# A fused two-block kernel on one core: value projection by channels with a turn behind it, one inverse application of 128 columns, an output turn in another bank, and a re-cut filling order

## Chip, cores, metric

One core of one Trainium2 chip. The metric is device time in microseconds (us) of one execution. Everything is float32.

## What is computed

The reference has a first block (an RWKV-7 layer, then a Hyena layer) and a second block (retention, differential attention and a gated MLP, two layers). The change touches the RWKV-7 layer alone. With 512 tokens (256 latent, 256 context) and 32 heads of 64 channels, cut to what matters here:

```python
proj = h @ w_in + (h_shift - h) @ (w_in * mu_cols)      # r, k, v, gate of 2048 channels each
kk = k * k_k; kk = kk / max(||kk||, 1e-12)              # per head of 64
# per head, in both directions z, one token after the other:
sa = s @ a_t                                            # a = -kk, b = kk * a
s  = s * w_t + sa b_t^T + v_t k_t^T
y  = s @ r_t
# both directions are added; then group norm per head, an affine, + bonus * v, * silu(gate)
```

The kernel evaluates the recurrence in chunks of 64 tokens. In a chunk, `sa` for all tokens is the solution of a triangular system whose 64x64 inverse is built by doubling.

## The kernel before

The layer runs as 16 rounds (`KE = 16`, called pairs here: one pair of heads, 128 channels, each). All engines' programs are written out by hand with semaphores; there is no planner. TensorE's program (`pairs_pe`) for pair `i` is a chain of small blocks in 64x64 tiles of the array, with full-array pieces for pair `i + 1` laid between them as fill:

- `first_blocks`, `low`, `full_blocks`: the chunk products; VectorE masks them (`start_inverse`, `mask_context`, `mask_tokens`).
- five levels of doubling: `below(l)` (64 matmul records in the trace), VectorE's `mask_level`, `grow(l)` (64 records), VectorE's `add_level`, then `turn_inverse` (DVE transposes) and ScalarE's `move_inverse`, and so to the next level. `seen_values` comes before the last `grow`.
- `solve`: the inverse times `W.AT` (the turned reads), then, in another group, times `W.X0` (the seen values): 32 matmuls of 64 columns each time. VectorE copies the first result (`weights`), ScalarE the second (`solved`).
- `transitions`, `own_states`, `own_reads`, then seven state steps `advance`/`read_states`, each round-tripping through VectorE and ScalarE (`state`).

The fill is the generator `between(i)`: it turns keys (`turn_keys`) and reads (`turn_reads`), projects the next pair's keys (8 matmuls of 512 columns), turns the previous pair's output (`turn_out`), and projects the next pair's values, reads and gates. `fill(part, columns)` takes pieces until their declared columns reach `columns`; the constants `FILL_*` say how much goes where. Each `pe.matmul` in float32 shows as two MATMUL records in the trace (8 key matmuls of 16 pairs: 256 records).

Values are projected with tokens as output rows: `mix_v` is the stationary operand and the weights are streamed, 32 matmuls of 128 columns (64 records) into bank 1. Bank 1 is also where `turn_out` puts the turned output of the pair before, which VectorE's `affine` reads; so `value_pieces` waits for `affine`. VectorE's `floor(m)` (the lower bound on the key norm, out of bank 0) stands behind the last `add_level`, and the first read piece waits for it because it writes bank 0.

DMA: each of the four weight slots (`w_k, w_v, w_r, w_g`, 512 KB) is refilled by the SP queue when its projection is done.

Of the kernel before, what the change touches and what calls it, by code (L numbers as in the profile page):

```python
# [14 lines left out]
P = 128  # L15
# [135 lines left out]
def rwkv_layer(nc, R, I, S):  # L151
# [19 lines left out]
    W.dif = hv[:, 6, :]  # L171
    W.late = [W.t1[0], W.dif]
    W.r, W.graw = hv[:, 7, 0:NX], hv[:, 7, NX:]
    W.t2 = [sv[:, 0, :], sv[:, 1, :]]
# [15 lines left out]
    W.Ax, W.Ac = sb("A_x", 2, 2, 4, P), sb("A_c", 2, 2, 4, HEAD)  # L190
    W.BK, W.AT, W.VZ = sb("BK", 2, NCH, P), sb("AT", 2, NCH, HEAD), sb("VZ", 2, NCH, P)
    W.T, W.U, W.Y, W.X0 = sb("T", 2, NCH, 64), sb("U", 2, NCH, 64), sb("Y", 2, NCH, 32), sb("X0", 2, NCH, 64)

# [193 lines left out]
def start_pool(pool, R, W, s):  # L387
# [32 lines left out]
LAST = 5  # L420
FILL_MASKS = 1000
FILL_BELOW = (0, 1000, 1000, 1000, 1100, 500)
FILL_GROWN = (0, 1200, 800, 800, 800, 800)
FILL_SEEN = 500
FILL_SOLVED = 500
FILL_MOVES = 500
# [98 lines left out]
def pairs_pe(pe, R, W, S, s, Z):  # L525
# [37 lines left out]
    def value_pieces(m):  # L563
        pe.wait_ge(s["w_v"], 16 * (m + 1))
        if m > 1:
            pe.wait_ge(s["affine"], 2 * (m - 1))
        if m == 0:
            pe.wait_ge(rate[1], 1)
            pe.wait_ge(s["mixed"], MIXED_V)
        for j in range(4):  # L570
            for k in range(KD):
                mm = pe.matmul(ps[:, 1, j * P:(j + 1) * P], W.mix_v[:, k, j * P:(j + 1) * P], W.wt[:, 1, k, :],  # L572
                               start=(k == 0), stop=(k == KD - 1))
                if k == KD - 1 and j == 3:
                    mm.then_inc(s["v_done"], 1)
                if k % 2:
                    yield

# [40 lines left out]

    def turn_out(i):  # L620
        pe.wait_ge(s["normed"], i + 1)
        pe.wait_ge(s["bonus_out"], i + 1)
        for j in range(2):
            pe.transpose(ps[:, 1, j * P:(j + 1) * P], W.ytok[:, j, :], R.eye[:, :])
        for j in range(2):
            mm = pe.transpose(ps[:, 1, NX + j * P:NX + (j + 1) * P], W.bonus[:, j, :], R.eye[:, :])
        mm.then_inc(s["turned"], 1)

    def bonus_weights(i):
# [4 lines left out]
        mm.then_inc(s["coef_done"], 1)  # L634

    def second_bank(i):
        if i + 1 < KE:
            pe.wait_ge(rate[1], i + 2)
        else:
            pe.wait_ge(s["g_out"], KE)  # L640

    def between(i):
        m = i + 1
        ahead = m < KE
        keys = key_pieces(m) if ahead else iter(())
        key = lambda: 512 if next(keys, None if not ahead else 1) is None else 0
        for z in range(2):
            for half in range(2):
                turn_keys(i, z, half)
                yield 290  # L650
            yield key()
        yield key()
        turn_reads(i)
        yield 640
        for _ in range(3):
            yield key()
        if i:
            second_bank(i)
            turn_out(i - 1)
# [7 lines left out]
        if not i:  # L667
            second_bank(i)
# [93 lines left out]
    def seen_values(i):  # L762
        for z in range(2):
            pe.wait_ge(v_in[z], i + 1)
            pe.wait_ge(at_out[z], i + 1)
        pe.wait_ge(s["coef_out"], i + 1)
        for j in range(4):
            for h in range(2):
                for p in range(2):
                    r, ch = nat(p), chunk_of(j, p)  # L770
                    for z in range(2):
                        g, n = solved_in(z, p), (4 * h + j) * 64
                        mm = pe.matmul(ps[g:g + 64, 6 + z, n:n + 64], strict(z, h, ch, r), W.VZ[r:r + 64, z, ch, rows(h)],
                                       start=True, stop=True)
                        if (j, h, p) == (3, 1, 1):
                            mm.then_inc(Z("x0_done")[z], 1)

    def solve(i, part):
        for z in range(2):
            pe.wait_ge(u_out[z], 6 * (i + 1))  # L780
        for n, right, done in ((0, W.AT, Z("wa_done")), (1, W.X0, Z("wu_done"))):
            if n:
                fill(part, FILL_SOLVED)
                for z in range(2):
                    pe.wait_ge(x0_out[z], i + 1)
            for j in range(4):
                for h in range(2):
                    for p in range(2):
                        a = oth(p)
                        for z in range(2):  # L790
                            g, q = solved_in(z, p), 4 * h + j
                            mm = pe.matmul(ps[a:a + 64, 2 + 2 * z + n, q * 64:q * 64 + 64], W.U[g:g + 64, z, q, :], right[g:g + 64, z, q, :],
                                           start=True, stop=True)
                            if (j, h, p) == (3, 1, 1):
                                mm.then_inc(done[z], 1)

# [67 lines left out]
    start_gate(pe, R, s, 2)  # L864
    start_gate(pe, R, s, 3)
    norm(0)
    for n, _ in enumerate(read_pieces(0)):
# [3 lines left out]
    for i in range(KE):  # L871
# [14 lines left out]
        for l in range(1, LAST + 1):  # L886
# [9 lines left out]
            fill(part, FILL_GROWN[l])  # L896
        solve(i, part)
        fill(part, FILL_SOLVED)
# [21 lines left out]
    pe.wait_ge(s["coef_out"], KE)  # L920
    turn_out(KE - 1)
    modulation_step(pe, R, S, 1, 1)


def pairs_act(act, R, W, s, Z):
# [45 lines left out]
    def root(m):  # L971
# [3 lines left out]
        act.activation(W.nrm, W.nrm, ACT.Exp, scale=-0.5).then_inc(s["root"], 1)  # L975

    def values(m):
        act.wait_ge(s["v_done"], m + 1)
# [23 lines left out]
    def reads_turned(i, z):  # L1002
        act.wait_ge(s["at_done1"], i + 1)
        act.activation(W.AT[:, z].rearrange("p (h j) n -> p h (j n)", h=2), ps[:, 6:8, z * NX:z * NX + NX], ACT.Copy).then_inc(Z("at_out")[z], 1)

# [7 lines left out]
    def seen(i, z):  # L1013
        act.wait_ge(Z("x0_done")[z], i + 1)
        if z:
            act.wait_ge(s["u_out1"], 6 * i + LAST)
        act.activation(W.X0[:, z].rearrange("p q n -> p (q n)"), ps[:, 6 + z, :], ACT.Copy).then_inc(Z("x0_out")[z], 1)

    def solved(i, z):
        act.wait_ge(Z("wu_done")[z], i + 1)  # L1020
        for p in range(2):
            g = slice(oth(p), oth(p) + 64)
            out = W.VZ[g, z].rearrange("p (j q) (h n) -> p h j q n", q=2, n=64)[:, :, :, p, :]
            src = ps[g, 3 + 2 * z, :].rearrange("p (h j n) -> p h j n", h=2, n=64)
            act.activation(out, src, ACT.Copy).then_inc(Z("u0_out")[z], 1)
# [25 lines left out]
    for z in range(2):  # L1051
        decays_early(0, z)
        decays_late(0, z)
    values(0)
    root(0)
    reads(0)
    gates(0)
    for i in range(KE):
# [32 lines left out]
        if ahead:  # L1091
            root(m)
        solved(i, 0)
        solved(i, 1)
# [12 lines left out]
def pairs_dve(dve, R, W, s, Z):  # L1107
# [100 lines left out]
    def weights(i, z):  # L1208
        dve.wait_ge(Z("wa_done")[z], i + 1)
        dve.tensor_copy(W.Wm[:, z].rearrange("p q n -> p (q n)"), ps[:, 2 + 2 * z, :]).then_inc(Z("w_out")[z], 1)  # L1210

# [39 lines left out]
    def affine(i):  # L1251
        vec = W.pv[:, i % 3, :]
        dve.wait_ge(s["turned"], i + 1)
        dve.tensor_scalar(W.yt, ps[:, 1, 0:NX], vec[:, V_LNW:V_LNW + 1], vec[:, V_LNB:V_LNB + 1], ALU.mult, ALU.add).then_inc(s["affine"], 1)
        dve.wait_ge(s["affine"], 2 * i + 1)
        dve.tensor_tensor(W.yt, W.yt, ps[:, 1, NX:], ALU.add).then_inc(s["affine"], 1)  # L1256

# [26 lines left out]
    for i in range(KE):  # L1284
# [9 lines left out]
        for l in range(1, LAST + 1):  # L1294
# [1848 lines left out]
```

## Time and profile before

| what | value |
|---|---|
| median of 3 runs | 2675.58 us (2672.11 to 2675.94) |
| profiled execution, its own time | 2679.32 us |
| its span, first to last instruction | 2677.5 us |
| mean granted TensorE clock | 0.988 of full speed |
| TensorE (PE) busy | 95% of the span |
| VectorE, ScalarE, GpSimd busy | 41%, 28%, 15% |
| the 16 pairs | from about 102 to 1076 us of the span |
| HBM read | 252.23 MB, 95 GB/s over the span |

Matmuls are pipelined and their ends are modelled, so a group's real cost is the distance from its start to the start of the next group, and "busy" overstates a little. A wait in brackets is idle time of the engine in front of the group and what ended it. "issue" is idle time that the profile puts down to nothing.

### The profile page before, as it was taken

The page shows a single profiled execution, that of the slowest core. Times are in us where ns is not written, and L with a number is a line of the kernel's source. Part 1 is how long each engine was busy: PE and PEld are TensorE (multiplying, and loading weights), DVE is VectorE, ACT ScalarE, POOL GpSimd, SP SyncE. Part 2 cuts the span into 40 slices and gives each one's busy share as a digit, 9 for nine tenths or more (in the row PEclk, how much of TensorE's full clock was granted, in tenths as well). Part 3 has the DMA queues.
Part 4 walks back from the last instruction along what each step waited for, and adds up shares of the span by engine and source line. Part 5 has one row for each costly group of instructions (what it writes and reads, how often), then busy time and mean ns, then how long its engine had stood idle before and what let it go on. Part 6 is the DMA issues. An engine that isn't in the chain of part 4 may idle for free.

```text
span 2677.5 us, 66401 instructions
## 1 busy us (share of the span) xinstructions
PE 2552.0 (95%) x29622; PEld 1768.1 (66%) x29622; DVE 1092.8 (41%) x2254; ACT 756.0 (28%) x1515; POOL 408.7 (15%) x439
## 2 busy tenths in 40 slices
PE   5999999999999997999999999999999999999998
PEld 1667777777777776558888764445544468775786
DVE  4655555655655554334463241104611113322512
ACT  3444444444444443131221220003400013102301
POOL 2433333333334331000001000000000001000000
PEclk8999999999999997999999999999999999999999
DMA  6211111111111102724445732220133353331352
GB/s 239 87 36 37 44 44 42 40 36 37 37 46 37 38 26 83 261 95 155 131 133 206 242 109 79 71 71 28 60 125 118 118 171 121 126 126 59 91 153 91
DMA packets 82065, 257.55 MB, mean 96 GB/s; under 512 B 11607, under 2 KB 19384, under 8 KB 81080
## 3 DMA queue, kind: packets, MB, share of 16 engines
q1 hardware_dynamic: 75176, 241.89, 27.6%
q10 hardware_dynamic: 6000, 8.28, 0.9%
q8 instruction: 236, 3.87, 0.6%
q0 software_dynamic: 608, 3.15, 0.3%
q14 instruction: 45, 0.37, 0.0%
HBM read 252.23 MB, written 1.05 MB: 95 GB/s over the span
## 4 chain that ended last, share of the span: by engine, by line
PE 57%; DVE 1%; ACT 1%; DMA 0%; issue 0%; SPq 0%; DVEq 0%; ACTq 0%
PE ps L1865 13%; PE ps L2034 9%; PE ps L1809 8%; PE ps L1745 7%; PE ps L2051 5%; PE ps L1899 4%; PE ps L1939 1%; PE ps L1690 1%; PE ps L1979 1%; PE ps L1959 1%; PE ps L1924 1%; PE ps L1766 1%; PE ps L1754 1%; PE ps L1919 1%; PE ps L1786 1%; PE ps L1842 1%
## 5 line engine op out<-in xcount | busy, mean ns | idle before, releaser
L1865 PE MATMUL ps<-h,ring 128*128 128x256 f32 (+1 forms) x1184 | 363.5, 465 | 0.0
L1865 PEld LDWEIGHTS ps<-h,ring 128*128 128x128 f32 x1184 | 225.0, 190 | 126.2 <-issue 107.1
L2034 PE MATMUL ps<-h,ring 128*128 128x512 f32 (+1 forms) x768 | 256.2, 486 | 0.0
L1809 PE MATMUL ps<-h,ring 128*128 128x256 f32 x1024 | 225.2, 379 | 0.8 <-ACT general L2197 0.8
L1809 PEld LDWEIGHTS ps<-h,ring 128*128 128x128 f32 x1024 | 193.9, 190 | 34.5 <-issue 7.7
L2034 PEld LDWEIGHTS ps<-h,ring 128*128 128x128 f32 x768 | 145.2, 190 | 103.0 <-issue 93.2
L1010 ACT ACTIVATE general<-general 64x512 f32<-64x512 f32 x160 | 100.8, 630 | 181.0 <-DVE general L1206 179.2
L572 PE MATMUL ps<-ring,general 128*128 128x128 f32 x1024 | 142.2, 285 | 6.5 <-DVE x L1256 6.5
L553 PE MATMUL ps<-general,ring 128*128 128x512 f32 x256 | 133.4, 617 | 0.8 <-issue 0.8
L2051 PE MATMUL ps<-general,ring 128*128 128x512 f32 (+1 forms) x384 | 131.0, 486 | 0.0
L572 PEld LDWEIGHTS ps<-ring,general 128*128 128x128 f32 x1024 | 122.5, 191 | 12.7 <-issue 8.6
L2945 POOL TENSOR_TENSOR h<-h,rstd 128x256 f32<-128x256 f32 x15 | 13.0, 881 | 762.1 <-ACT rstd L2168 762.1
L2352 ACT ACTIVATE general<-ps 128x512 f32<-128x512 f32 (+1 forms) x48 | 23.2, 491 | 330.9 <-PE ps L2034 330.9
L1745 PE MATMUL ps<-general,ring 128*128 128x256 f32 x512 | 114.2, 381 | 1.5 <-PEq L77 1.5
L736 PEld LDWEIGHTS ps<-general 64*64 64x64 f32 (+1 forms) x5120 | 79.2, 131 | 51.5 <-issue 45.8
L1745 PEld LDWEIGHTS ps<-general,ring 128*128 128x128 f32 x512 | 96.4, 190 | 23.6 <-issue 10.1
L1899 PE MATMUL ps<-ring,h 128*128 128x512 f32 x256 | 110.2, 592 | 0.0
L2051 PEld LDWEIGHTS ps<-general,ring 128*128 128x128 f32 x384 | 73.0, 190 | 50.9 <-issue 45.9
L1206 DVE STREAM_TRANSPOSE general<-general 128x512 f32<-128x512 f32 x160 | 104.3, 690 | 2.2
L736 PE MATMUL ps<-general 64*64 64x32 f32 (+1 forms) x5120 | 88.7, 218 | 12.6 <-issue 10.8
L2823 DVE TENSOR_TENSOR general<-ps,general 128x512 f32<-128x512 f32 (+1 forms) x32 | 17.9, 558 | 199.7 <-PE ps L2051 199.7
L751 PEld LDWEIGHTS ps<-general 64*64 64x64 f32 x4096 | 68.7, 139 | 41.0 <-issue 35.6
(355 smaller groups left out, 4063.7 us busy)
## 6 DMA issues: line engine op xcount, KB each, us to landing
ring<-in_w_mods SPq DMA_DIRECT2D x96, 512.0 KB, 5.2
ring<-in_w_feature SPq DMA_DIRECT2D x74, 512.0 KB, 3.4
ring<-in_w_rkvg SPq DMA_DIRECT2D x64, 512.0 KB, 3.7
ring<-in_w_in SPq DMA_DIRECT2D x48, 512.0 KB, 3.5
ring<-in_w_merge SPq DMA_DIRECT2D x48, 512.0 KB, 3.5
ring<-in_w_out SPq DMA_DIRECT2D x32, 512.0 KB, 5.4
ring<-in_w_token SPq DMA_DIRECT2D x24, 512.0 KB, 3.9
ring<-in_w_merge SPq DMA_DIRECT2D x48, 256.0 KB, 3.0
```

The source lines that it names most:

```text
L553: mm = pe.matmul(ps[:, 0, :], W.wt[:, 0, k, :], W.mix_k[:, k, :], start=(k == 0), stop=(k == KD - 1))
L572: mm = pe.matmul(ps[:, 1, j * P:(j + 1) * P], W.mix_v[:, k, j * P:(j + 1) * P], W.wt[:, 1, k, :], start=(k == 0), stop=(k == KD - 1))
L736: mm = pe.matmul(ps[own, b0 + h, j * P:j * P + 32], left, right, start=True, stop=True)
L751: mm = pe.matmul(ps[a:a + 64, b0 + h, j * P:j * P + 32], W.U[g:g + 64, z, q, :], W.Y[g:g + 64, z, q, :], start=True, stop=True)
L1010: last = act.activation(W.U[g:g + 64, 1], W.X0[a:a + 64, 1], ACT.Copy)
L1206: dve.transpose(out, W.T[:, z]).then_inc(done, 1)
L1745: mm = pe.matmul(ps[:, n % 3, 0:NX], weights(key, k % 8), rhs(k), start=(k == 0), stop=(k == K - 1))
L1809: mm = pe.matmul(ps[:, n % 4, 0:NX], weights(key, k), R.h[:, k, 0:NX], start=(k == 0), stop=(k == KD - 1))
L1865: mm = pe.matmul(ps[:, j % 4, 0:width], weights(("feature", l, j), k), R.h[:, k, cols], start=(k == 0), stop=(k == KD - 1))
L1899: mm = pe.matmul(ps[:, (GAP + n) % 4, :], R.h[:, k, t * P:(t + 1) * P], weights(("token", l, g, k // 2), k % 2, 512), start=(k == 0), stop ...
L2034: mm = pe.matmul(ps[:, 2 * b, 0:NQ], weights(key, k), R.h[:, k, 0:NQ], start=(k == 0), stop=(k == KD - 1))
L2051: mm = pe.matmul(ps[:, 2 * b + 1, 0:NQ], weights(key, k), W.F[:, 4 * (RG, MG, DG)[b] + k, 0:NQ], start=(k == 0), stop=(k == KB - 1))
```

## The change

1. `value_pieces` projects by channels, as keys are: weights stationary, `mix_v` streamed, 8 matmuls of 512 columns, waiting only for the rates to be read out of bank 1. ScalarE copies the result (`values_raw`, 128x512) into a spare tile, TensorE turns it (`turn_values`, 4 transposes) back into bank 1, and `values` copies it as before.
2. `W.AT` and `W.X0` become the two halves of one tile `W.AX` of 128 columns; `solve` applies the inverse once, 32 matmuls of 128 columns. `weights` and `solved` read their halves, and `solved` also waits for `weights`.
3. `turn_out` writes bank 6 instead of bank 1 (bank 1 in the last pair); `affine` reads there; `seen_values` waits for `affine` in place of `value_pieces`.
4. `floor(m)` goes in front of the last `add_level`.
5. Two of the four key turns of direction 0 go between the two `full_blocks` (`FILL_TOKENS`); the other fill constants are cut anew.

```diff
-FILL_MASKS = 1000
-FILL_BELOW = (0, 1000, 1000, 1000, 1100, 500)
-FILL_GROWN = (0, 1200, 800, 800, 800, 800)
+FILL_TOKENS = 500
+FILL_MASKS = 500
+FILL_BELOW = (0, 1000, 1000, 1000, 1000, 500)
+FILL_GROWN = (0, 1200, 800, 500, 500, 1000)
-FILL_SOLVED = 500
+FILL_SOLVED = 600
...
     def value_pieces(m):
         pe.wait_ge(s["w_v"], 16 * (m + 1))
-        if m > 1:
-            pe.wait_ge(s["affine"], 2 * (m - 1))
+        pe.wait_ge(rate[1], m + 1)
         if m == 0:
-            pe.wait_ge(rate[1], 1)
             pe.wait_ge(s["mixed"], MIXED_V)
-        for j in range(4):
-            for k in range(KD):
-                mm = pe.matmul(ps[:, 1, j * P:(j + 1) * P], W.mix_v[:, k, j * P:(j + 1) * P], W.wt[:, 1, k, :],
-                               start=(k == 0), stop=(k == KD - 1))
...
+        for k in range(KD):
+            mm = pe.matmul(ps[:, 1, :], W.wt[:, 1, k, :], W.mix_v[:, k, :], start=(k == 0), stop=(k == KD - 1))
+            if k == KD - 1:
+                mm.then_inc(s["v_done"], 1)
+            yield
+
+    def turn_values(m):
+        pe.wait_ge(s["v_raw"], m + 1)
         for j in range(4):
+            mm = pe.transpose(ps[:, 1, j * P:(j + 1) * P], W.vraw[:, j * P:(j + 1) * P], R.eye[:, :])
+        mm.then_inc(s["v_turned"], 1)
...
-        for n, _ in enumerate(value_pieces(m)):
-            yield 290
-            if n == 6:
+        for n, _ in enumerate(value_pieces(m)):
+            yield 512
+            if n == 3:
                 norm(m)
                 yield 512
-        for _ in read_pieces(m):
+        for n, _ in enumerate(read_pieces(m)):
             yield 256
+            if n == 3:
+                turn_values(m)
+                yield 290
...
-    def solve(i, part):
+    def solve(i):
         for z in range(2):
             pe.wait_ge(u_out[z], 6 * (i + 1))
-        for n, right, done in ((0, W.AT, Z("wa_done")), (1, W.X0, Z("wu_done"))):
-            if n:
-                fill(part, FILL_SOLVED)
-                for z in range(2):
-                    pe.wait_ge(x0_out[z], i + 1)
...
+            pe.wait_ge(x0_out[z], i + 1)
+        for j in range(4):
+            for h in range(2):
+                for p in range(2):
+                    a = oth(p)
+                    for z in range(2):
+                        g, q = solved_in(z, p), 4 * h + j
+                        mm = pe.matmul(ps[a:a + 64, 2 + 2 * z + h, j * P:(j + 1) * P], W.U[g:g + 64, z, q, :], W.AX[g:g + 64, z, q, :],
+                                       start=True, stop=True)
...
         if i + 1 < KE:
             low(i + 1, 1)
+        fill(part, FILL_TOKENS)
         full_blocks(i, 1)
...
+    def values_raw(m):
+        act.wait_ge(s["v_done"], m + 1)
+        act.wait_ge(s["cum1"], m + 1)
+        act.activation(W.vraw, ps[:, 1, :], ACT.Copy).then_inc(s["v_raw"], 1)
...
     def solved(i, z):
+        act.wait_ge(Z("w_out")[z], i + 1)
         act.wait_ge(Z("wu_done")[z], i + 1)
...
         if ahead:
             root(m)
+            values_raw(m)
         solved(i, 0)
...
+            if l == LAST and ahead:
+                floor(m)
             for z in range(2):
                 add_level(i, z, l)
         if ahead:
-            floor(m)
             pack_keys(m, 0)
```

## Rows read from the trace of the kernel before

**Rows 1.** The page, part 1: busy time, share and instructions of each engine.
```profile
PE 2552.0 (95%) x29622; PEld 1768.1 (66%) x29622; DVE 1092.8 (41%) x2254; ACT 756.0 (28%) x1515; POOL 408.7 (15%) x439
```

**Rows 2.** Waits of PE, 60 to 1100 us: total, times, longest.
```profile
PE ps L714 <- DVE general L1179: 11.6, 16, 1.8
PE ps L736 <- issue: 10.8, 8, 2.2
PE ps L585 <- DVE h L1129: 9.5, 15, 1.6
PE ps L572 <- DVE x L1256: 6.5, 14, 0.5
PE ps L841 <- DVE general L1231: 4.9, 20, 0.5
```

**Rows 3.** Windows, each from a pair's first `low` to the next's; last the 16th pair.
```profile
165.99:227.67 61.68, 58.38 (x1473) 44.27 (x1467) 35.28 (x74) 27.60 (x54) 21.65 (x22) 1.00 0.14 40
...
288.30:348.04 59.74, 57.77 (x1470) 43.95 (x1467) 35.12 (x73) 27.11 (x53) 21.66 (x22) 1.00 0.14 41
...
712.04:775.42 63.38, 59.87 (x1472) 45.08 (x1466) 35.45 (x74) 27.76 (x54) 21.65 (x22) 0.97 0.13 38
...
895.85:957.11 61.26, 58.23 (x1471) 44.12 (x1467) 35.28 (x74) 27.60 (x54) 21.65 (x22) 1.00 0.14 40
1016.00:1084.00 68.00, 46.43 (x1377) 39.49 (x1378) 29.04 (x67) 20.19 (x39) 11.19 (x11) 0.77 0.26 80
```

**Rows 4.** Timeline of PE before the first pair: start, us, line, shape, records.
```profile
72.05 7.10 PE L553 MATMUL ps<-general,ring 128*128 128x512 f32 x16 [0.83 <-issue]
...
80.90 7.41 PE L572 MATMUL ps<-ring,general 128*128 128x128 f32 x64
```

**Rows 5.** Timeline of PE in the 8th pair (i = 7).
```profile
535.19 1.16 PE L714 MATMUL ps<-general 64*128 64x128 f32 x16 [0.67 <-DVE general L1179]
536.28 1.09 PE L605 MATMUL ps<-eye,general 128*128 128x128 f32 x8
537.21 1.02 PE L553 MATMUL ps<-general,ring 128*128 128x512 f32 x2
538.16 1.14 PE L736 MATMUL ps<-general 64*64 64x32 f32 x64
...
554.48 1.14 PE L751 MATMUL ps<-general 64*64 64x32 f32 x64
555.55 1.60 PE L572 MATMUL ps<-ring,general 128*128 128x128 f32 x12
557.08 0.88 PE L736 MATMUL ps<-general 64*64 64x32 f32 x43
...
570.52 0.67 PE L585 MATMUL ps<-general,ring 128*128 128x256 f32 x2 [0.56 <-DVE h L1129]
571.12 1.16 PE L792 MATMUL ps<-general 64*64 64x64 f32 x64
572.22 1.13 PE L585 MATMUL ps<-general,ring 128*128 128x256 f32 x4
```

**Rows 6.** Timeline of DVE in the same pair.
```profile
536.40 1.29 DVE L1179 TENSOR_TENSOR general<-ps,x 128x512 f32<-128x512 f32 x2 [1.26 <-PE ps L714]
...
555.67 0.75 DVE L1191 TENSOR_TENSOR general<-general,ps 128x256 f32<-128x256 f32 x2 [1.87 <-PE ps L751]
...
568.91 0.88 DVE L1197 SCALAR_TENSOR_TENSOR general<-ps,x,general 128x256 f32<-128x256 f32 x2 [3.20 <-PE ps L757]
569.70 0.68 DVE L1129 TENSOR_SCALAR h<-ps 128x512 f32<-128x512 f32 x1
```

**Rows 7.** Timeline of ACT in the same pair.
```profile
557.20 1.27 ACT L1010 ACTIVATE general<-general 64x512 f32<-64x512 f32 x2 [3.51 <-DVE general L1206]
...
574.49 2.45 ACT L1025 ACTIVATE general<-ps 64x512 f32<-64x512 f32 x4 [2.78 <-PE ps L792]
```

**Rows 8.** DMA queues, 160 to 1000 us: packets, MB, share of 16 engines.
```profile
q8 instruction: 160, 2.62, 1.3%
```

More of the change, by code:

```diff
@@ L172, in rwkv_layer @@
     W.late = [W.t1[0], W.dif]
+    W.vraw = W.t1[1]
     W.r, W.graw = hv[:, 7, 0:NX], hv[:, 7, NX:]
@@ L190, in rwkv_layer @@
     W.Ax, W.Ac = sb("A_x", 2, 2, 4, P), sb("A_c", 2, 2, 4, HEAD)
-    W.BK, W.AT, W.VZ = sb("BK", 2, NCH, P), sb("AT", 2, NCH, HEAD), sb("VZ", 2, NCH, P)
-    W.T, W.U, W.Y, W.X0 = sb("T", 2, NCH, 64), sb("U", 2, NCH, 64), sb("Y", 2, NCH, 32), sb("X0", 2, NCH, 64)
+    W.BK, W.AX, W.VZ = sb("BK", 2, NCH, P), sb("reads_seen", 2, NCH, P), sb("VZ", 2, NCH, P)
+    W.T, W.U, W.Y = sb("T", 2, NCH, 64), sb("U", 2, NCH, 64), sb("Y", 2, NCH, 32)
+    W.AT, W.X0 = W.AX[:, :, :, 0:HEAD], W.AX[:, :, :, HEAD:]
     W.Wm = W.T
@@ L618, in turn_reads, with turn_out @@
             mm.then_inc(Z("at_done")[z], 1)
-    def turn_out(i):
+    def turn_out(i, bank):
         pe.wait_ge(s["normed"], i + 1)
@@ L623, in turn_out @@
         for j in range(2):
-            pe.transpose(ps[:, 1, j * P:(j + 1) * P], W.ytok[:, j, :], R.eye[:, :])
+            pe.transpose(ps[:, bank, j * P:(j + 1) * P], W.ytok[:, j, :], R.eye[:, :])
         for j in range(2):
-            mm = pe.transpose(ps[:, 1, NX + j * P:NX + (j + 1) * P], W.bonus[:, j, :], R.eye[:, :])
+            mm = pe.transpose(ps[:, bank, NX + j * P:NX + (j + 1) * P], W.bonus[:, j, :], R.eye[:, :])
         mm.then_inc(s["turned"], 1)
@@ L634, in bonus_weights @@
         mm.then_inc(s["coef_done"], 1)
[L636 to L640, printed above, removed]
     def between(i):
@@ L657, in between @@
         if i:
-            second_bank(i)
-            turn_out(i - 1)
+            pe.wait_ge(at_out[1], i + 1)
+            turn_out(i - 1, 6)
             yield 290
@@ L766, in seen_values @@
         pe.wait_ge(s["coef_out"], i + 1)
+        if i:
+            pe.wait_ge(s["affine"], 2 * i)
         for j in range(4):
@@ L776, in seen_values @@
                             mm.then_inc(Z("x0_done")[z], 1)
-    def solve(i, part):
+    def solve(i):
         for z in range(2):
             pe.wait_ge(u_out[z], 6 * (i + 1))
-        for n, right, done in ((0, W.AT, Z("wa_done")), (1, W.X0, Z("wu_done"))):
-            if n:
-                fill(part, FILL_SOLVED)
-                for z in range(2):
-                    pe.wait_ge(x0_out[z], i + 1)
-            for j in range(4):
[L787 to L795, printed above, removed]
+            pe.wait_ge(x0_out[z], i + 1)
[7 more added lines that the diff above has]
+                                       start=True, stop=True)
+                        if (j, h, p) == (3, 1, 1):
+                            mm.then_inc(Z("wu_done")[z], 1)
     def transitions(i, z):
@@ L865, in pairs_pe @@
     start_gate(pe, R, s, 3)
+    turn_values(0)
     norm(0)
@@ L896, in pairs_pe @@
             fill(part, FILL_GROWN[l])
-        solve(i, part)
+        solve(i)
         fill(part, FILL_SOLVED)
@@ L920, in pairs_pe @@
     pe.wait_ge(s["coef_out"], KE)
-    turn_out(KE - 1)
+    turn_out(KE - 1, 1)
     modulation_step(pe, R, S, 1, 1)
@@ L1053, in pairs_act @@
         decays_late(0, z)
+    values_raw(0)
     values(0)
@@ L1208, in weights @@
     def weights(i, z):
-        dve.wait_ge(Z("wa_done")[z], i + 1)
-        dve.tensor_copy(W.Wm[:, z].rearrange("p q n -> p (q n)"), ps[:, 2 + 2 * z, :]).then_inc(Z("w_out")[z], 1)
+        dve.wait_ge(Z("wu_done")[z], i + 1)
+        dve.tensor_copy(W.Wm[:, z], two_banks(2 + 2 * z)[:, :, 0:64]).then_inc(Z("w_out")[z], 1)
     def moves(i, z):
@@ L1251, in affine @@
     def affine(i):
-        vec = W.pv[:, i % 3, :]
+        vec, bank = W.pv[:, i % 3, :], 6 if i < KE - 1 else 1
         dve.wait_ge(s["turned"], i + 1)
-        dve.tensor_scalar(W.yt, ps[:, 1, 0:NX], vec[:, V_LNW:V_LNW + 1], vec[:, V_LNB:V_LNB + 1], ALU.mult, ALU.add).then_inc(s["affine"], 1)
+        dve.tensor_scalar(W.yt, ps[:, bank, 0:NX], vec[:, V_LNW:V_LNW + 1], vec[:, V_LNB:V_LNB + 1], ALU.mult, ALU.add).then_inc(s["affine"], 1)
         dve.wait_ge(s["affine"], 2 * i + 1)
-        dve.tensor_tensor(W.yt, W.yt, ps[:, 1, NX:], ALU.add).then_inc(s["affine"], 1)
+        dve.tensor_tensor(W.yt, W.yt, ps[:, bank, NX:], ALU.add).then_inc(s["affine"], 1)
     def bonus_weights(i):
```

14 lines of the change are left out of this document (4 added, 10 removed), and 2 rows, old and new, of the table PAIR_SEMS.

## The prediction

> **What bounds the kernel now.** I read the engines' shares first: PE is busy 95% of the span and no other engine over 41% [rows 1], so only PE's own work and PE's waits count. The change lies in the 16 pairs, so next the windows by pair: 13 of them from 165.99 to 957.11 us take 60.9 us on average, the shortest 59.74 and the longest 63.38, at full clock but for the longest (0.97), while the last pair, which has nothing to fill with, stands at 0.77 [rows 3]. Then who PE waits for [rows 2]: per pair it is three short waits on VectorE that this change aims at (L714 on the masks, L585 on the floor, L572 on the affine), a little in the state steps (L841), and an irregular wait put down to "issue". The rest of a pair is PE work laid end to end, so the work itself has to be priced, from distances between starts [rows 4, 5].
>
> **Values.** Now 64 records of 128 columns; uninterrupted they took 7.41 us, 116 ns each. The same number of products in the key form, 16 records of 512 columns, took 7.10 us, 444 ns each [rows 4]. Change: -0.31 us. Four transposes (8 records) are new; eight such records take 537.21 - 536.28 = 0.93 us [rows 5]: +0.93. So the projection by itself is a loss of 0.62 us per pair. What it can win is elsewhere: fewer, longer pieces, and ScalarE's additional 128x512 copy (about 0.6 us) goes on an engine 28% busy.
>
> **Switches between array shapes.** Twelve value records between two tiled groups took 557.08 - 555.55 = 1.53 us against 12 x 0.116 = 1.39 [rows 4, 5]: 0.14 per full-array stretch. Working through the generator with the old and the new fill constants, I count 21 such stretches before and 22 after (the key turns get one of their own between the full blocks, the norm one after the fourth `grow`; the stretch inside `solve` goes). +0.15.
>
> **Solve.** Now 2 x 1.10 us (571.12 to 572.22 for 64 records of 64 columns) [rows 5], 17.2 ns a record. After, 64 records of 128 columns. From below: the record rate stays, 1.10 us. From above: a record costs twice as much, 2.20 us, no gain. Between: a full-array record of 128 columns takes 116 ns [rows 4] and four 64x64 tiles work at once (64 columns need half of that, 58 ns, yet a record ends every 17.2 ns, so more than three do), giving 116/4 = 29 ns and 1.86 us; I take 1.9, -0.3. Tiled groups of 32 columns cost the same 1.07 us for 64 records (554.48 to 555.55) [rows 5], so up to 64 columns something other than streaming sets the rate, and 128 is past it.
>
> The Trainium skill (TensorEngine Tiling (Array Packing), Instruction Overhead) says each matmul has about 60 cycles of overhead, so that one column costs what sixty do. By that rule 64 columns already lie at the end of the flat part and 128 cost twice as much: solve stays at 2.2 us. The equal 32- and 64-column groups agree with its flat part; nothing in this trace shows 128 columns in a 64x64 tile. The sum would be 0.3 us per pair smaller in gain; it is the second case below.
>
> **The three waits.** (a) Floor. PE waits 0.56 us for VectorE's L1129, which ran 569.70 to 570.38 behind `add_level` [rows 5, 6]. In front of it, it runs while VectorE idles 3.20 us for the last `grow` [rows 6]. The next thing late is `add_level` itself, which `solve` needs: done 0.88 us after it takes up the last `grow` (568.91 to 569.79). In the new order two value pieces, 1.9 us, lie between. Gone: -0.56. (b) Affine: 6.5 us over 14 pairs [rows 2], -0.46. It moves to `seen_values`, two levels (over 8 us) later, covered. (c) Masks: 0.67 us before the second `full_blocks` [rows 5]. Two key turns (0.93) now fill it, so PE starts that block at 534.52 + 0.93 = 535.45, 0.26 us later than now. VectorE's mask of it ends 2.50 us after its start (535.19 to 537.69) [rows 5, 6], hence at 537.95, and the first `below` waits for that; it starts now at 538.16. Two thirds of the wait comes back as a new wait of about 0.45 in front of `below(1)`: -0.2 only.
>
> **State steps.** The generator now leaves eight gate pieces for the steps where five were, so `advance(4)` is covered too. L841's waits are 4.9 us in all [rows 2]: between 0 and -0.35 per pair, I take -0.2.
>
> **What could become late.** With one value piece (1.05) where three were (1.5), `below(4)` starts 1.07 + 1.05 = 2.12 us after `grow(3)`; VectorE is done 556.42 - 554.48 = 1.94 after it [rows 5, 6]. Margin 0.18. The same holds for `below(5)`, with the norm as cover. `grow(4)` needs ScalarE's move, 558.47, 3.99 us after `grow(3)` [rows 7]; it now starts 5.1 after. `solve` also needs the seen values out; by the same count they are 1.9 us early. `weights` (two 128x512 copies out of PSUM, 0.68 us each by L1129's) [rows 6] now waits for the whole solve; `transitions` needs the first, 0.7 us after solve, under three read pieces of 1.5 us. ScalarE's `solved`, 2.45 us for four copies [rows 7], starts 0.7 after solve and has its first direction done 1.3 later; `own_states(0)` comes some 4 us after solve. ScalarE's queue: `values_raw` stands in front of `solved`, but its projection ends before solve begins; `values` stands in front of the states, and `turn_values` is issued right after the first `transitions`, before them. No DMA is added; the weight refills for keys and values keep their place within 3 us of now, that for gates comes some 2 us later in the pair, with over 40 us to spare.
>
> **Sum.** Per full pair -0.31 + 0.93 + 0.15 - 0.30 - 0.56 - 0.46 - 0.20 - 0.20 = -0.95 us. Times 14: -13.3. Before the first pair the projection and turn stand bare: +0.6. The first pair has no affine wait but the longest floor wait (1.6) [rows 2]: -1.6. The last has the longest mask wait (1.8) [rows 2], of which the turns take half: -0.8. In all -15.1: the profiled execution's 2679.3 becomes 2664.2 and, as the median lies 3.7 below that execution, 2660.5 is the forecast.
>
> **Issue waits.** The 13 windows exceed 59.74 by 14.5 us in sum. Part of it is the "issue" wait. In the window the instruction queue moved 160 packets, 2.62 MB [rows 8], 16 KB each, 12 per pair. My reading is that a block is late when its transfer meets a weight refill: in the middle pairs the longest of these waits come in every third pair, inside `below(4)` (L736) [rows 2], after the keys' slot begins to be refilled. The Trainium skill (Runtime: NRT & Kernel Launch, Instruction fetch mechanics) says that the instruction memory is refilled in 16 KiB blocks of 256 instructions; the trace agrees (2.62 MB / 160). A pair now has 104 matmul records fewer of 1473, 7%, so the phase moves and these waits will fall in other pairs and places. I cost it at nothing; the bounds are all gone (-15) or every pair as dear as the longest.
>
> **Rivals.**
> Likeliest (0.58): the sum, 2650 to 2668.
> Second, solve gains nothing and the state steps give nothing: -0.95 + 0.5 = -0.45 per pair, some -8 in all: 2668. The flat 32/64 rows speak for it, the four tiles at once against it. 0.14.
> Third, the change of waits does not do what it says: each of the two thin covers (0.18 us) misses by 0.4 to 0.5 and the affine wait returns in `seen_values`. Then -0.95 + 0.95 = 0: 2675. 0.10.
> Fourth, other side: instruction blocks. If the fill between `grow(3)` and `grow(5)`, now poorer in time by about 2.5 us per pair, lets the late block hit every pair as at 712.04 (63.38 with the clock at 0.97, 3.6 over the shortest) [rows 3], instead of 1.1 on average, that adds 2.5 x 15 = 37: 2698. It decides from 1.0 us more per pair on. Fewer instructions speak against it, the last pair (densest, clock 0.77) for it. 0.08.
> Fifth, the blocks fall well, or the last pair keeps its clock: 8 to 15 more: 2648. 0.10.
>
> **Range and chances.** 2646 to 2672 holds the first, second and fifth cases. A difference under 0.2% (5.4 us) can't be told from none in this kernel. Faster by more: the first and fifth and most of the second, 0.78; within: the rest of the second and the third, 0.13; slower: 0.09.
>
> **What would show it.** Right: L585's wait on the floor and the value pieces' wait on the affine are gone; a wait of about 0.45 us stands before `below(1)`; value stretches of 16 records a pair sum to about 7.9 us; solve 1.9 us; shortest pair about 58.8. Wrong: solve at 2.2, waits on `add_level` before `below(4)` or `below(5)`, "issue" waits above 1 us per pair, ScalarE waiting at `values` with the states behind it.

## The result, and the profile after

The changed kernel takes 2636.52 us (median of 4 runs, 2632.17 to 2638.04) against 2675.76 for the kernel before: ratio 0.9852, 95% interval 0.984 to 0.9863, 39 us faster. The forecast was 2660.5 and the range's lower end was 2646. The direction was right, the size was 2.6 times too small. The profiled execution took 2635.36 us against 2679.32, so the traces hold 44.0 us to find.

The page of the changed kernel, part 1. PE stays the bound, with 1728 matmul records fewer [rows 1].
```profile
PE 2535.8 (96%) x27894; PEld 1682.7 (64%) x27894; DVE 1090.9 (41%) x2254; ACT 766.1 (29%) x1531; POOL 408.3 (16%) x439
```
Its instruction queue between 160 and 1000 us. ([rows 8] counts from 165 us on; between 160 and 1000 us it is 161 packets and 2.64 MB.)
```profile
q8 instruction: 156, 2.56, 1.2%
```

PE's two largest waits in the changed kernel, 60 to 1100 us, as [rows 2]: total, times, longest.
```profile
PE ps L735 <- DVE general L1186: 7.9, 16, 1.5
PE ps L838 <- DVE general L1238: 4.7, 18, 0.4
```
The floor wait and the affine wait are gone. What is left of the three is the wait of the first `below` (L735) for the masks, 0.43 us a pair.

Windows of the changed kernel: the first pair, the shortest middle pair, and the 13 middle pairs in one (columns as [rows 3]; the sixth entry behind the length is the granted clock).
```profile
104.53:162.10 57.57, 56.80 (x1360) 38.73 (x1354) 33.58 (x70) 27.77 (x52) 19.57 (x20) 1.00 0.16 51
337.99:395.86 57.87, 57.10 (x1366) 38.82 (x1359) 35.17 (x74) 28.26 (x55) 21.65 (x22) 1.00 0.13 42
162.10:922.79 760.69, 745.78 (x17660) 506.39 (x17654) 457.34 (x950) 367.56 (x703) 281.26 (x286) 1.00 0.13 41
```
The same for the kernel before; the shortest middle pair is in [rows 3]. The second row is the part of its first pair around the end of its longest floor wait (141.78 us).
```profile
102.72:165.99 63.27, 58.46 (x1469) 44.76 (x1463) 33.98 (x70) 27.35 (x51) 19.57 (x20) 0.97 0.15 46
140.00:146.00 6.00, 4.35 (x68) 3.15 (x58) 2.77 (x5) 1.26 (x2) 2.24 (x2) 0.72 0.28 90
165.99:957.11 791.12, 757.54 (x19064) 574.27 (x19059) 459.06 (x950) 358.85 (x690) 281.56 (x286) 1.00 0.14 40
```
The second row's clock is a mean: TensorE was granted its lower level of 1.2 GHz from 142.1 to 145.5 us and its full 2.4 GHz around it.

So an undisturbed middle pair, the shortest of 13, went from 59.74 to 57.87 us (-1.87, forecast -0.95). "Excess" below is what 13 middle pairs take beyond 13 times the shortest: 791.12 - 776.62 = 14.5 us before, 760.69 - 752.31 = 8.4 after. The 44 us of this pair of profiles divide so (a second pair of profiles, further down, has the same pairs and another start and end):

| stretch | forecast | measured |
|---|---|---|
| start to the first `low` | +0.6 | +1.8 |
| first pair | -1.6 | -5.7 |
| 13 middle pairs, undisturbed part | -12.4 | -24.3 |
| 13 middle pairs, excess | 0 | -6.1 |
| last two pairs | -1.7 | -8.9 |
| all behind | 0 | -0.7 |

The timeline of PE in a middle pair of the changed kernel, from the last part of the projection on, answers to [rows 5].
```profile
426.99 0.76 PE L735 MATMUL ps<-general 64*32 64x32 f32 x64
427.68 1.12 PE L572 MATMUL ps<-general,ring 128*128 128x512 f32 x2
428.73 1.16 PE L774 MATMUL ps<-general 64*64 64x64 f32 x64
429.82 1.13 PE L572 MATMUL ps<-general,ring 128*128 128x512 f32 x2
430.88 0.75 PE L756 MATMUL ps<-general 32*32 32x32 f32 x64
431.56 1.98 PE L572 MATMUL ps<-general,ring 128*128 128x512 f32 x4
433.48 1.98 PE L789 MATMUL ps<-general 64*64 64x128 f32 x64
435.39 1.56 PE L589 MATMUL ps<-general,ring 128*128 128x256 f32 x6
...
438.27 0.60 PE L580 MATMUL ps<-eye,h 128*128 128x128 f32 x4
438.80 1.04 PE L819 MATMUL ps<-general 128*64 128x64 f32 x28
```
Three things are read here. Solve takes 435.39 - 433.48 = 1.91 us (forecast 1.9). The four turns of the values (L580) are 4 records, 438.80 - 438.27 = 0.53 us, not 8 records and 0.93. And no wait stands in front of solve: the last value pieces cover `add_level`, and the read pieces, which need the floor, come behind solve.

The same can be done for a whole undisturbed pair: the distance from each record's start to the next one's, idle time kept apart, added up by what the records do. Before (288.30 to 348.04 us) against after (337.99 to 395.86 us), in us a pair:

| term of the forecast | forecast | before | after | measured |
|---|---|---|---|---|
| values, projection | -0.31 | 8.46 | 8.03 | -0.43 |
| values, turn | +0.93 | 0 | 0.53 | +0.53 |
| switches between shapes (all other groups together) | +0.15 | | | -0.15 |
| solve | -0.30 | 2.18 | 1.91 | -0.27 |
| three waits, as idle time | -1.22 | 1.69 | 0.43 | -1.26 |
| state steps with their waits | -0.20 | 3.99 | 3.69 | -0.30 |

The sum is -1.88, which is the -1.87 of the windows to 0.01.

### The profile page after: what moved, and what is told of

Same layout as the page of the kernel before. It is cut to its first block, busy times and chain, and to the rows that moved or that the text cites. A ratio compares the mean times of both kernels' runs of the same rounds, so it can differ in the third digit from the quotient of the medians.

```text
span 2633.6 us, 63024 instructions
## 1 busy us (share of the span) xinstructions
PE 2535.8 (96%) x27894; PEld 1682.7 (64%) x27894; DVE 1090.9 (41%) x2254; ACT 766.1 (29%) x1531; POOL 408.3 (16%) x439
## 4 chain that ended last, share of the span: by engine, by line
PE 57%; DVE 1%; ACT 1%; ACTq 1%; DMA 0%; issue 0%; SPq 0%; DVEq 0%
PE ps L1873 14%; PE ps L2042 9%; PE ps L1817 8%; PE ps L1753 6%; PE ps L2059 5%; PE ps L1907 4%; PE ps L1947 1%; PE ps L1698 1%; PE ps L1987 1%; PE ps L1967 1%; PE ps L1932 1%; PE ps L1774 1%; PE ps L1927 1%; PE ps L1762 1%; PE ps L1794 1%; ACTq L2367 1%
## 5 line engine op out<-in xcount | busy, mean ns | idle before, releaser
L556 PE MATMUL ps<-general,ring 128*128 128x512 f32 x256 | 134.9, 623 | 0.8 <-issue 0.8
L572 PE MATMUL ps<-general,ring 128*128 128x512 f32 x256 | 134.2, 629 | 0.0
L735 PEld LDWEIGHTS ps<-general 64*64 64x64 f32 (+1 forms) x5120 | 79.4, 133 | 68.1 <-issue 43.2
L735 PE MATMUL ps<-general 64*64 64x32 f32 (+1 forms) x5120 | 88.0, 218 | 10.1 <-DVE general L1186 7.9
L2462 DVE COPY h<-ps 128x256 f32<-128x256 f32 x40 | 17.0, 424 | 190.7 <-PE ps L1753 190.6
```

The source lines that it names most:

```text
L556: mm = pe.matmul(ps[:, 0, :], W.wt[:, 0, k, :], W.mix_k[:, k, :], start=(k == 0), stop=(k == KD - 1))
L572: mm = pe.matmul(ps[:, 1, :], W.wt[:, 1, k, :], W.mix_v[:, k, :], start=(k == 0), stop=(k == KD - 1))
L735: mm = pe.matmul(ps[own, b0 + h, j * P:j * P + 32], left, right, start=True, stop=True)
```

## The experiments

Each run has its own profile. In the fences of waits the largest rows are shown. "Undisturbed pair" is the shortest of the 13 middle ones; ratios are to the kernel before, measured beside it.

**The changed kernel with one part undone (four runs on one chip).**

Values by tokens:
```diff
-        for k in range(KD):
-            mm = pe.matmul(ps[:, 1, :], W.wt[:, 1, k, :], W.mix_v[:, k, :], ...)
+        for j in range(4):
+            for k in range(KD):
+                mm = pe.matmul(ps[:, 1, j * P:(j + 1) * P], W.mix_v[:, k, j * P:(j + 1) * P], W.wt[:, 1, k, :], ...)
-                turn_values(m)
```


> The changed kernel with its values projected as before (32 matmuls of 128 columns, tokens as output rows, no copy and no turn), everything else as changed. Theory A (every part is worth what its records cost): the token form costs 8.38 us a pair in the kernel before, the channel form 8.05 plus 0.53 for the four turns plus 0.1 for the norm standing alone, so the undisturbed pair (57.87 us in the changed kernel) becomes 0.2 to 0.3 us shorter or stays, and the whole time stays within 0.2% of the changed kernel, near 2634 us. Rival B (the channel form is what brought the surprise, through fewer records and fewer instruction blocks): the issue waits come back to those of the kernel before, 0.5 us a pair more, and the time is 7 to 10 us above the changed kernel, near 2645 us.

Measured: 2645.26 us, ratio 0.9886 (0.9869 to 0.9904). The undisturbed pair is 57.69 us, 0.18 shorter than in the changed kernel; but the 13 middle pairs take 766.20, excess 16.2 against 8.4. Waits of PE in this kernel, 160 to 930 us:
```profile
PE ps L735 <- DVE general L1183: 5.6, 13, 0.4
PE ps L702 <- issue: 3.6, 4, 1.2
PE ps L838 <- DVE general L1235: 3.4, 14, 0.2
PE ps L573 <- issue: 3.1, 4, 1.2
PE ps L774 <- issue: 2.1, 3, 0.8
PE ps L756 <- issue: 1.1, 2, 0.6
```
Both theories had half of it: by its work the token form is the shorter one, as theory A had it, and it loses all the same, by issue waits, as B had it. Over the 13 middle pairs the issue waits are 5.1 us in the changed kernel and 11.0 here. The medians are 9 us apart; the middle pairs account for 5.5 of it, and the rest lies in the start and the last stretch, which wander from execution to execution (the last table of this section).

Solve in two groups:
```diff
-                        mm = pe.matmul(ps[...], W.U[g:g + 64, z, q, :], W.AX[g:g + 64, z, q, :], ...)
+        for n, right in ((0, W.AT), (1, W.X0)):
+            if n:
+                fill(part, FILL_SOLVED)
```


> The changed kernel with the inverse applied in two groups of 64 columns, with a fill stretch between, as before. Theory A: 2.19 us in place of 1.91, and one more full-array stretch (0.15): the undisturbed pair is 0.4 us longer, the 14 full pairs 6 us, and the last pair about 1: 2643 us. Rival B (the solve's 64 records fewer are what shortened the last pair by 7.6 us, and thinned the issue waits): the last pair (first blocks to the end of its state steps, 52.7 us in the changed kernel) is 3 us or more longer, the issue waits 0.3 us a pair more, 2650 us.

Measured: 2651.54 us, ratio 0.9912 (0.9897 to 0.9927), 15 above the changed kernel; in the trace 14.7. The undisturbed pair is 58.43, 0.56 longer; the 13 middle pairs take 6.6 us more, the first pair is 2.8 longer (60.40, 1.0 of it an issue wait), the stretch from the last `low` to the modulation matmuls after the pairs 2.9, and 2.2 lie behind it. Excess 7.7, issue waits 3.1 us: not more than in the changed kernel. Theory A had the place right and the size low; B's issue waits did not come. Of the 0.56 us, start to start, 0.27 is solve (2.18 against 1.91) and 0.30 is in the state steps (3.99 against 3.69): the stretch inside solve takes three read pieces, so the last gate stretch in the state steps has 2 records in place of 4. The number of full-array stretches does not change: 22 in either trace.

Floor behind `add_level`:
```diff
-            if l == LAST and ahead:
-                floor(m)
             for z in range(2):
                 add_level(i, z, l)
         if ahead:
+            floor(m)
```


> The changed kernel with the floor behind the last add_level again. Theory A (the floor wait went because the piece that needs it now comes after solve, whatever the floor's place): no wait on the floor, undisturbed pair 57.9 us, time as the changed kernel within 0.1%. Rival: the floor's place did it: 0.56 to 0.63 us a pair come back, in the first read piece or through weights waiting behind the later root and unit keys, 2645 us.

Measured: 2641.13 us, ratio 0.9875 (0.986 to 0.9889; the changed kernel's is 0.984 to 0.9863). The undisturbed pair is 57.87, as in the changed kernel, and the 13 middle pairs take 760.45 against 760.69. Theory A holds for them: with the fill re-cut they have no floor wait, wherever the floor stands. Only the first pair needs the move: 59.46 against 57.57, with a wait of 0.61 us on the floor. The time is 4.6 us above the changed kernel's, more than the 0.1% that theory A allowed: in the traces, 3.0 us apart, 1.9 of it is the first pair and the rest lies outside the middle pairs.

Output turned in bank 1:
```diff
+        if m > 1:
+            pe.wait_ge(s["affine"], 2 * (m - 1))     # in value_pieces
-            turn_out(i - 1, 6)
+            turn_out(i - 1, 1)
```


> The changed kernel with the output turned in bank 1 again, so that the value pieces wait for affine. Theory A: the wait returns with its real cost, 0.61 us a pair from start to start (0.46 as the profile shows it), 14 times: undisturbed pair 58.5, time 8 us above the changed kernel, 2644 us. Rival: with value pieces of 1.05 us in place of 0.6 the wait is partly covered, 0.3 us a pair or less, 2640 us.

Measured: 2644.78 us, ratio 0.9894 (0.9877 to 0.991), undisturbed pair 58.45. Theory A: +0.58 us a pair. Waits of PE in this kernel, 160 to 930 us: the profile shows 6.0 us over 13 pairs, 0.46 each, as in [rows 2], where the pair pays 0.58.
```profile
PE ps L574 <- DVE x L1266: 6.0, 13, 0.5
PE ps L740 <- DVE general L1189: 5.6, 13, 0.4
```

**The kernel before with the moves alone.** Floor, bank 6 and the two key turns between the full blocks; projection, solve and the other constants as before.
```diff
+            if l == LAST and ahead:
+                floor(m)
...
+            turn_out(i - 1, 6)
...
+        fill(part, FILL_TOKENS)      # 500, and FILL_MASKS 500
         full_blocks(i, 1)
```


> The kernel before with only the moves: floor in front of the last add_level, output turned in bank 6, two key turns between the full blocks; projection, solve and the other fill constants as before. Theory A: affine wait -0.61, mask wait -0.25, and the read piece in front of solve starts when the last value piece ends, floor wait -0.63 with nothing late behind it, so undisturbed pair 59.75 - 1.5 = 58.3, and in the first pair the 1.65 us wait and the clock drop behind it gone (-3): 2675 - 14 x 1.5 - 3 = 2651 us. Rival (the waits move on): in old fill order the state steps and add_level waits grow, under 0.7 us a pair won, 2665 us.

Measured: 2659.38 us, ratio 0.9934 (0.9917 to 0.995). Undisturbed pair 58.43, that is -1.31 of the -1.87, with no floor wait and no affine wait left: in the old filling order the moves do remove them. First pair 60.04 (-3.2), at clock 1.00. Excess 15.9 us, issue waits 9.6 against 7.3 before, with the same 1466 records a pair. The time is 8 us above theory A's 2651 and below the rival's 2665. Its windows, first pair and shortest:
```profile
104.70:164.74 60.04, 57.41 (x1469) 44.10 (x1462) 33.89 (x70) 27.24 (x51) 19.58 (x20) 1.00 0.17 49
700.67:759.10 58.43, 57.73 (x1472) 43.97 (x1467) 35.27 (x74) 27.49 (x54) 21.68 (x22) 1.00 0.14 42
```
With the run above on solve the undisturbed pair closes: moves -1.31, solve in one group -0.56 (0.30 of it in the state steps), and for projection, turn, norm and the rest of the re-cut fill together 0.00. The three moves were not undone one by one in this kernel.

**Without weight loads.** Each 512 KB load after the first pair is cut to 4 bytes, at the same place and with the same semaphores (60 loads; the later pairs compute with the first pair's weights).
```diff
-  sp.dma_start(R.ring[:, n, :], I["w_rkvg"][m, :, n * D:(n + 1) * D])
+  rows_, cols_ = (P, D) if m == 0 else (1, 1)
+  sp.dma_start(R.ring[0:rows_, n, 0:cols_], I["w_rkvg"][m, 0:rows_, n * D:n * D + cols_])
```
The kernel before:


> The kernel before, with 4 bytes in place of each 512 KB weight load of the pairs after the first (it computes with the first pair's weights; left out are 60 loads). Theory C (the issue waits in the pairs are instruction blocks late behind a weight load): they are gone from the middle pairs, each takes 59.75 us, and the 13 windows lose their 14 us: 2661 us. Rival (PE drains the instructions faster than they come, whatever else moves, or the waits are of another kind): the waits stay in place, 2675 us.

Measured: 2665.57 us, ratio 0.9961 (0.9946 to 0.9975). Undisturbed pair 59.69, excess 3.7 in place of 14.5, issue waits 0.8 in place of 7.3; the wait in every third pair is gone. The first pair takes 61.80 us, with the same waits as before (4.66 us against 4.65, the floor's 1.65 among them) and the clock at 1.00 throughout. PE's waits, 160 to 1000 us:
```profile
PE ps L715 <- DVE general L1180: 9.2, 14, 0.7
PE ps L586 <- DVE h L1130: 7.9, 14, 0.6
PE ps L573 <- DVE x L1257: 6.5, 14, 0.5
PE ps L842 <- DVE general L1232: 3.5, 15, 0.5
PE ps L704 <- issue: 0.8, 3, 0.3
```
The changed kernel:


> The changed kernel, with the same loads cut to 4 bytes. Theory C: its issue waits are gone too, each middle pair takes 57.87 us, 8 us less over the 13 windows than the changed kernel, 2628 us; the difference to the kernel before without loads is then the pure change of work and waits, 1.88 us a pair. Rival: no change against the changed kernel, 2636 us.

Measured: 2634.99 us, ratio 0.9845 (0.9826 to 0.9863), no faster than the changed kernel. Undisturbed pair 57.86, excess 5.9 against 8.4, issue waits 2.8 against 5.1; the 13 middle pairs are 2.7 us shorter and the last stretch 5.1 longer (115.5). Theory C explains three quarters of the excess before and less than a third of what is left after.

The values by tokens:


> The run with values projected by tokens (e1), with 4 bytes in place of each weight load after the first pair (it computes with the first pair's weights). Undisturbed pair 57.7 as there. If the 11.0 us of issue waits that the token form has over 13 pairs come from instruction blocks that meet weight loads, they fall below 3 us and the excess from 16 to about 5, time 2633 us, level with the changed kernel without loads (2635). If they come from the number of instructions alone, they stay and the time stays near 2645.

Measured: 2637.88 us, ratio 0.9848 (0.9827 to 0.9869). Excess 7.1 against 16.2, issue waits 3.3 against 11.0. Nine of its sixteen us of excess come from the loads, and without loads it is level with the changed kernel (2634.99), as the first reading expected, if not quite as far: 3.3 us of issue waits stay where under 3 were foretold, and the excess is 7.1 and not 5.

Are the issue waits late instruction blocks? The packet times of the traces say so. In the twelve profiles of the kernels so far and of the repeats below there are 103 issue waits in the middle pairs, and 102 of them end 1.1 to 1.6 us after a 16 KB packet of the instruction queue has ended. Such a packet comes about every 5 us, so a moment taken at random lies so in one case of ten. In both profiles of the kernel before, all 22 such waits had a weight load's packets moving in the 3 us before that instruction packet or beside it, where one instruction packet in three has (52 and 51 of 152). The packet itself is no slower: ahead of the five longest waits at L736 in the first profile it took 0.9 to 1.0 us, where the median is 1.0. What is late is its start. In the changed kernel 3 of 10 such waits, and with values by tokens 7 of 15, had no weight load near.

**One step on.** Both free key pieces in front of the first `below`.
```diff
-            yield key()
+            if z == 0:
+                yield key()
+                yield key()
...
-FILL_MASKS = 500
+FILL_MASKS = 1000
```


> A step on: the changed kernel with both free key pieces of the first half laid in front of the first below (fill 1000 in place of 500), into the 0.43 us wait for the masks. Theory A: the wait (0.5 from start to start) is covered, later levels have over 0.9 us of room, so 0.4 to 0.5 us a pair: 57.4, and 2630 us. Rival: the piece is missed in a later level or in the state steps and the wait comes back there: 2636 us.

Measured: 2637.46 us, ratio 0.9852 (0.9835 to 0.9869), no gain in time. The 13 middle pairs are 5.2 us shorter (755.49), and the last stretch, 116.1 against 110.4, took that back. The undisturbed pair is 57.65, not 57.4: the mask wait is gone and a new one stands at the norm, on GpSimd. PE's waits, 160 to 930 us:
```profile
PE ps L840 <- DVE general L1240: 4.7, 13, 0.4
PE ps L564 <- POOL h L1391: 3.0, 13, 0.2
PE ps L704 <- issue: 2.4, 3, 1.0
```
Then the norm one value piece later (`if n == 4` for `if n == 3`):


> The run with the second key piece (e8), with the norm one value piece later, so that it no longer waits 0.23 us for GpSimd's square in each pair. If the fixed costs of a pair are all that counts: undisturbed pair 57.65 - 0.23 = 57.42 us, 14 pairs, 6 us under the changed kernel: near 2631 us. Rival (what a pair gains in fixed costs is within what the issue waits and the last pair move from kernel to kernel): the undisturbed pair is 57.42, but the time is within 3 us of the changed kernel.

Measured: 2632.65 us, ratio 0.9835 (0.9817 to 0.9854), undisturbed pair 57.43, 13 middle pairs 752.09 (760.69 and, below, 759.59 in the changed kernel). Its median is the lowest of all: its four times are 2631.95 to 2637.13, those of the changed kernel on the same chip 2636.16 to 2641.18. The intervals of the two ratios overlap a little, so the 6 us are likely, not certain; the shorter middle pairs are in the trace.

**Both kernels once more**, for what belongs to the program and what to one execution.

> The changed kernel once more, with its own profile, to see how much of the issue waits and of the last pair belongs to the program and how much to one execution. If to the program: excess of the 13 middle pairs over 57.87 each near 8.4 us again, issue waits at the same places, last stretch (last low to the modulation after the pairs) near 110.4 us. If to the execution: either moves by several us, and only the undisturbed pair (57.87) stays.

> The kernel before once more, with its own profile. If the program decides: excess over 59.74 near 14.5 us, a wait in every third pair in below(4), last stretch near 119 us, as in its first profile. If the execution decides: these move by several us, and the difference between the two kernels' profiles that is not in the undisturbed pair (20 of 44 us) is partly chance.

| | shortest pair | 13 middle pairs | issue waits in them | first pair | last `low` to the modulation |
|---|---|---|---|---|---|
| before | 59.74 | 791.12 | 7.3 | 63.27 | 119.3 |
| before again | 59.91 | 791.00 | 7.8 | 63.27 | 114.5 |
| changed | 57.87 | 760.69 | 5.1 | 57.57 | 110.4 |
| changed again | 57.86 | 759.59 | 4.4 | 57.57 | 111.3 |

The times: 2638.85 us for the changed kernel, ratio 0.9855 (0.9837 to 0.9872), and 2678.88 for the one before, 1.0001 (0.9989 to 1.0014). The middle and first pairs are the program's, to about 1 us in 790; the last stretch is not: 4.7 us between two executions of one program. Nor is the start: the first `low` stands at 104.53 and 102.16 us in the changed kernel's two profiles, at 102.72 and 103.97 in the other's.

## Why the forecast was too small

Of the 29 us that the forecast lacks against the profiles, 12 are in the sum for one undisturbed pair, 6 in the issue waits of the middle pairs, 4 in the first pair, 7 in the last two pairs and 1 behind them, less 1 at the start. The last three are within what executions of one program differ by; the first three are the steps that failed.

**What held.** PE is the bound throughout. The direction of the projection's price was right (-0.43 in the pair, -0.31 foretold), and so was that the projection with its turn wins nothing by itself: 0.18 us a pair lost against the token form. The mask wait came back as forecast: 0.43 us by the profile in front of the first `below`, with 0.45 foretold. Solve takes 1.91 us. The count of full-array stretches is right, 21 before and 22 after in the traces. The thin covers of 0.18 us in front of the fourth and fifth `below` held; no wait stands there. Nothing new waits on ScalarE.

**The turn of the values (+0.93): mis-sized.** I took a transpose for two records, as a float32 matmul has. It has one: the 8 records of [rows 5] were the eight transposes of two key turns (all that direction 0 has). This is the largest mis-sized term of the pair. Four cost 0.53. Over 14 pairs that is 5.6 us.

**Switches (+0.15): mis-sized, with the wrong sign.** The term counted stretches, and one stretch more was right. But groups changed their price by what stands beside them: reads and gates fell by 0.31, in eight stretches where nine held them, bonus weights by 0.14 and `low` by 0.07, while keys rose by 0.17, key turns by 0.09 and the norm by 0.10. Together -0.15, 0.30 less than forecast.

**Solve and state steps (-0.30, -0.20): right, and a little short.** Solve's own -0.27 is as forecast. The state steps gave 0.30, by shorter groups and not by shorter waits: the bracketed waits there are 0.28 before and 0.34 after. The run with solve in two groups gives both back, which is why it costs 0.56.

**The waits (-1.22): right.** -1.26 as idle time, -1.31 by the run with the moves alone. The affine wait cost 0.58 where its bracket showed 0.46, so its bracket was too low a price. For the floor the move was enough in the old filling order, but in the middle pairs of the changed kernel it was not needed: with the read pieces behind solve the wait goes without it, which the forecast did not see.

So the undisturbed pair went by -1.87 where I had -0.95, which over 13 pairs is 12 of the missing 29 us. This is the step that failed most (the second pair of profiles has -2.05): the turn priced at twice its records (0.40 a pair) and the switches (0.30) make up most of it.

**Issue waits (costed at nothing): the second step that failed.** My bounds were "all gone" and "every pair as dear as the longest", and I took the middle of them as no change. The excess of the middle pairs fell by 6 us (14.5 to 8.4, and 14.4 to 7.4 in the second profiles, both against 59.74 and 57.86; against the second profile's own shortest pair, 59.91, it would be 12.2). That these waits in the kernel before come with the weight loads is shown by the run without loads (14.5 to 3.7), and that the channel form is what thins them by the run with tokens (8.4 to 16.2, and 7.1 without loads). The four profiles with loads and values by tokens (both of the kernel before, the moves alone, the first run above) have 7.3 to 11.0 us of issue waits in the middle pairs, the four with loads and values by channels among the runs that undo a part or repeat the kernel have 3.1 to 4.8, the changed kernel 5.1. The channel form pays here and nowhere else: 7.8 us of excess in the trace, for a form that costs 0.18 us a pair more of work. Why it does so is open. The smaller number of instructions looks like the reason, but the runs speak against the mere count: with solve in two groups a pair has 1422 records and 3.1 us of issue waits, with values by tokens 1402 records and 11.0. Where the records stand must matter; 64 short records in the value stretches in place of 16 long ones would ask for the next block sooner there, but no run tests that alone. Nor is all of the excess issue wait: in the longest pair [rows 3] the granted clock fell to 1.2 GHz right behind the wait of 1.56 us. What makes the 3.7 to 7 us of excess that stay without loads is open.

**The first pair (-1.6): terms missed.** It gave 5.7 in both pairs of profiles. Besides the floor wait of 1.65 us there was a wait of 1.2 for the values' read-out, and between them TensorE's granted clock was 0.72 in the mean over 140 to 146 us (1.2 GHz from 142.1 to 145.5); in the changed kernel it is 1.00 throughout. All waits of the pair fell from 4.65 to 0.63 us. The clock is priced by the run of the kernel before without loads, which has the same 4.66 us of waits and no fall of the clock: 61.80 against 63.27, that is 1.5. So 4.0 and 1.5 of the 5.7 are found. That run also shows that the wait alone does not bring the clock down; it fell in both profiles of the kernel before, and what decides it is open. I had read the row of the pair and not its clock, and counted one wait of four kinds.

**The last two pairs (-1.7): mostly not to be forecast.** -8.9 in the first pair of profiles, -3.2 in the second. With solve in two groups the stretch was 2.9 us longer than in the first profile of the changed kernel and 2.0 longer than in the second, which is less than the 4.7 that one program's executions differ by, so no part of it is shown to be solve's. The last pair runs at a mean clock of 0.75 before and 0.75 and 0.72 after, so my fifth case (it keeps its clock) did not come about.

**The chances.** The time lies beyond my fifth case, whose 8 to 15 us were the right kind and came on top of a sum that was itself too small. Errors on one side, in the sum, the issue waits and the first pair, were not allowed for together.

## What to carry to other kernels

When PE is 95% busy with short groups in changing tile shapes, price a change by start-to-start distances, and check on a row with a known count how many records one instruction has before multiplying. The affine wait cost 0.12 us more than its bracket; so measure a wait's price across it, from start to start. A wait that was covered by re-ordering needs no second cure. Idle time that the profile ascribes to nothing is not noise: where it repeats with the program, look at whether it ends just behind a packet of the instruction queue, and whether large loads move beside it. A form with fewer, longer instructions may then gain more than its work, as here; the count of instructions over the whole round did not foretell it.

## What the runs showed of the hardware

- A float32 transpose of 128x128 is one matmul record, 0.53 us for four between two read pieces and a tiled group; a float32 matmul is two records.
- In 64x64 tiles, 64 records take 1.07 us with 32 columns, 1.10 with 64 and 1.91 with 128: the rate is flat to 64 columns and then 30 ns a record, not twice 17. The rule of the Trainium skill (TensorEngine Tiling (Array Packing), Instruction Overhead), by which 128 columns would have cost 2.2 us, agrees with the flat part and is too dear at 128.
- Instruction blocks were late by up to 1.6 us beside 512 KB weight loads in the middle pairs of the kernel before, and by 0.3 us at most with the loads cut. In the changed kernel and in the form with values by tokens, waits of up to 0.8 and 1.0 us stay without loads. The Trainium skill (Runtime: NRT & Kernel Launch, Instruction fetch mechanics) calls the cost of a block boundary mostly hidden; in the middle pairs before, that is so for 141 of 152 blocks, and the other 11 showed as 7.3 us of waits.
